# A decoder step on one core: cache pages loaded as rows of two tokens, two pages over the two halves of the partitions

## The reference, cut to what matters

```python
k_past = cache_k[l, page_table].reshape(db, past, N_HEADS, HEAD_DIM)
v_past = cache_v[l, page_table].reshape(db, past, N_HEADS, HEAD_DIM)
f_past = cache_logf[l, page_table].reshape(db, past, N_HEADS)
...
s = jnp.einsum('bqhd,bkhd->bhqk', q, k) * (HEAD_DIM ** -0.5)
s = s + c_q[...] - c_k[...]          # c = cumsum(logf) over the tokens
p = jax.nn.softmax(s, axis=-1)
o = jnp.einsum('bhqk,bkhd->bqhd', p, v)
```

## Time and profile before

| | |
|---|---|
| median of 3 runs | 2878.92 us (2878.82 to 2878.99) |
| the profiled execution | 2883.59 us, its span 2881.9 us |
| PE busy | 2639.3 us, 92% of the span |
| VectorE, ScalarE, GpSimd busy | 1429.0, 731.3 and 141.6 us |
| moved by DMA | 532.93 MB, mean 185 GB/s |
| granted TensorE clock, mean | 0.941 |

### The profile page before, as it was taken

How to read it: one execution, slowest core, us unless ns; L and a number is a source line. 1 busy time by engine, 2 the same in 40 slices (tenths; PEclk the granted TensorE clock), 3 DMA queues, 4 the chain that set the end, 5 groups by cost and what they waited for, 6 DMA issues and landing times.

```text
span 2881.9 us, 50518 instructions
## 1 busy us (share of the span) xinstructions
PE 2639.3 (92%) x19656; PEld 2326.1 (81%) x19656; DVE 1429.0 (50%) x5629; ACT 731.3 (25%) x979; POOL 141.6 (5%) x289
## 2 busy tenths in 40 slices
PE   5899899964767879998999999999999999999998
PEld 3799889851323336676999999999999999999998
DVE  4786777769777142225343434434343434343433
ACT  4332122212223341123222222222222222222221
POOL 0100000001111112200000000000000000000000
PEclk8999999985676899997999999999999999999999
DMA  6789899987999977735222222232222222322221
GB/s 238 243 290 333 315 337 343 328 302 277 359 371 359 338 263 262 250 121 174 90 89 88 88 88 89 102 103 90 88 88 89 89 89 101 104 89 88 89 88 63
DMA packets 274530, 532.93 MB, mean 185 GB/s; under 512 B 16410, under 2 KB 177787, under 8 KB 272980
## 3 DMA queue, kind: packets, MB, share of 16 engines
q1 hardware_dynamic: 218605, 376.20, 37.8%
q0 software_dynamic: 35440, 127.78, 12.1%
q10 hardware_dynamic: 20247, 25.73, 2.6%
HBM read 503.94 MB, written 24.05 MB: 183 GB/s over the span
## 4 chain that ended last, share of the span: by engine, by line
PE 77%; DMA 9%; DVE 9%; issue 2%; ACT 1%; SPq 1%; POOL 0%; POOLq 0%; ACTq 0%; DVEq 0%
PE ps L707 76%; DMA t_r<-in_cache_k 6%; DVE t_work L1777 6%; DMA t_r<-in_cache_v 1%; DMA t_wraw<-in_w_in 1%; PE ps L710 1%; DVE t_wl L1614 0%; ACT t_wh L1227 0%; DVE t_work L1614 0%; DMA t_auxW<-in_pool_w 0%; DMA t_wraw<-in_w_o 0%; DVE t_xl L1614 0%; DVE t_auxW L1614 0%; SPq L577 0%; DVE t_nmax L1915 0%
## 5 line engine op out<-in xcount | busy, mean ns | idle before, releaser
L707 PE MATMUL ps<-t_xh,t_wh 128*128 128x260 f32 (+1 forms) x4352 | 949.8, 293 | 15.4 <-DVE t_xl L1614 15.3
L707 PE MATMUL ps<-t_xh,t_wl 128*128 128x260 f32 (+1 forms) x4352 | 936.5, 291 | 0.0
L707 PE MATMUL ps<-t_xl,t_wh 128*128 128x260 f32 (+1 forms) x4352 | 935.2, 291 | 0.0
L1614 DVE TENSOR_TENSOR t_wl<-t_wraw,t_wh 128x1024 fp32r<-128x1024 f32 x376 | 460.4, 1225 | 890.9 <-ACT t_wh L1227 890.9
L1227 ACT ACTIVATE t_wh<-t_wraw 128x1024 fp32r<-128x1024 f32 x376 | 398.0, 1060 | 1654.0 <-PE ps L707 1653.8
L707 PEld LDWEIGHTS ps<-t_xh,t_wh 128*128 128x128 f32 x4352 | 685.8, 190 | 96.1 <-issue 66.2
L707 PEld LDWEIGHTS ps<-t_xh,t_wl 128*128 128x128 f32 x4352 | 686.1, 190 | 11.8
L707 PEld LDWEIGHTS ps<-t_xl,t_wh 128*128 128x128 f32 x4352 | 685.5, 190 | 8.9
L1777 DVE CUSTOM_DVE_ANT_0 t_work<-t_r,t_work 128x128 f32<-128x128 f32 x2048 | 455.2, 287 | 134.3 <-DMA t_r<-in_cache_k 121.9
L707 PE MATMUL ps<-t_hh,t_wh 128*128 128x260 f32 x1408 | 285.6, 284 | 3.4 <-issue 3.4
L707 PE MATMUL ps<-t_hh,t_wl 128*128 128x260 f32 x1408 | 284.5, 284 | 0.0
(11 more groups left out here) (256 smaller groups left out, 1205.8 us busy)
## 6 DMA issues: line engine op xcount, KB each, us to landing
t_r<-in_cache_k SPq DMA_DIRECT2D x256, 512.0 KB, 6.9
t_r<-in_cache_v POOLq DMA_DIRECT2D x228, 512.0 KB, 6.7
t_wraw<-in_w_up SPq DMA_DIRECT2D x44, 2048.0 KB, 8.0
t_wraw<-in_w_in SPq DMA_DIRECT2D x22, 2048.0 KB, 9.6
t_wraw<-in_w_down SPq DMA_DIRECT2D x22, 2048.0 KB, 7.8
t_wraw<-in_w_o SPq DMA_DIRECT2D x11, 2048.0 KB, 10.6
t_r<-in_cache_v SPq DMA_DIRECT2D x28, 512.0 KB, 6.8
scr_proj<-t_stg ACTq DMA_DIRECT2D x40, 256.0 KB, 4.6
```

The costliest lines, as they stand in the source:

```text
L707: return pe.matmul(out, lhsT, rhs, start=start, stop=stop)
L1614: return dve.tensor_tensor(out, in0, in1, op)
```

## The change

A page's 128 tokens are now seen as 64 rows of 8 KB, tokens 2q and 2q + 1 in row q (`rows_of_page`). Page n goes to 64 partitions: the lower half when its buffer's number is even, the upper half when it is odd; its 8 KB fill two neighbouring ring buffers on those partitions (`half_page`). So an even and an odd page together fill the two buffers that held them before, and a partition's first buffer holds even tokens, its second odd ones, of one page in the lower half, of the other in the upper half. Both consumers still take 128 partitions of one buffer at a time; for that both pages must have landed, and a pair's buffers are free only when both have been used. The waits follow: the consumer of an even page waits for both loads (`key_page`, `value_page`), and both loads of a pair wait for the two uses of the pair before (`key_load`, `value_places`). `biases_full` writes the biases in the same order, by four matmuls of 64 x 64 in place of a transpose. POOL waits for `x_spilled` before its first value page. Numbers, sizes and order of the loads are as before.

```diff
-    for n in range(DEC * PAGES):
+    for n in range(0, DEC * PAGES, 2):
         b = n % (2 * RING if K_END[-1] < slot_of[n] < TAIL else RING)
-        loads[b] += 1
-        places.append((b, loads[b], held.get(b, -1)))
-        held[b] = n
+        for i in range(2):
+            loads[b + i] += 1
+            places.append((b + i, loads[b + i], held.get(b, -1)))
+        held[b] = n + 1
...
+        def rows_of_page(pages, g):
+            return pages[bass.ds(g, 1), :, :].rearrange("a (q j) n -> (a q) j n", j=2)
+
+        def half_page(ring, b):
+            return ring[64 * (b % 2):64 * (b % 2) + 64, b - b % 2:b - b % 2 + 2, :]
...
                     pool.wait_ge(v_used, held + 1 + PRIME)
-                    pool.dma_start(vring[:, b, :],
-                                   v_pages[bass.ds(g, 1), :, :].rearrange("a p n -> (a p) n")).then_inc(v_loaded[b], 16)
+                    pool.dma_start(half_page(vring, b), rows_of_page(v_pages, g)).then_inc(v_loaded[b], 16)
+
+            pool.wait_ge(x_spilled, 16)
...
-            def page(ring, pages, loads, used, g, r, p):
-                sp.wait_ge(used, r * PAGES + (p + 1))
-                sp.dma_start(ring[:, p % RING, :],
-                             pages[bass.ds(g, 1), :, :].rearrange("a p n -> (a p) n")).then_inc(loads[p % RING], 16)
+            def key_load(g, n):
+                sp.wait_ge(k_used, n + 2 - n % 2)
+                sp.dma_start(half_page(kring, n % RING), rows_of_page(k_pages, g)).then_inc(k_loaded[n % RING], 16)
...
-                        last = tr(ps[:, 4 + i % 2, n * P:(n + 1) * P], lfE[:, c, h, :], P)
+                        for j in range(2):
+                            for b in range(2):
+                                last = mm(ps[64 * b:64 * b + 64, 4 + i % 2, n * P + j:(n + 1) * P:2],
+                                          lfE[:, c, h, j::2], ident[:, b::2])
...
             def value_page(r, p):
                 b, load, _ = V_PLACES[r * PAGES + p]
-                pe.wait_ge((v_loaded + k_loaded)[b], 16 * load)
+                if p % 2 == 0:
+                    for i in range(2):
+                        pe.wait_ge((v_loaded + k_loaded)[b + i], 16 * load)
...
             def key_page(r, p):
-                dve.wait_ge(k_loaded[p % RING], r * (16 * PAGES // RING) + 16 * (p // RING + 1))
+                if p % 2 == 0:
+                    for i in range(2):
+                        dve.wait_ge(k_loaded[p % RING + i], r * (16 * PAGES // RING) + 16 * (p // RING + 1))
```

More of the change, by code:

```diff
@@ L93, in value_places @@
     places, held, loads = [], {}, [0] * RING + [DEC * PAGES // RING] * RING
-    for n in range(DEC * PAGES):
+    for n in range(0, DEC * PAGES, 2):
         b = n % (2 * RING if K_END[-1] < slot_of[n] < TAIL else RING)
-        loads[b] += 1
-        places.append((b, loads[b], held.get(b, -1)))
-        held[b] = n
-    return places, max(held.get(b, -1) for b in range(RING, 2 * RING)), loads
+        for i in range(2):
+            loads[b + i] += 1
+            places.append((b + i, loads[b + i], held.get(b, -1)))
+        held[b] = n + 1
+    return places, max(held.get(b, -1) for b in range(RING, 2 * RING, 2)), loads
 V_PLACES, V_WIDE, V_LOADS = value_places()
@@ L632, in _ @@
                 for n, g in zip(kp, kg):
-                    page(kring, k_pages, k_loaded, k_used, g, *divmod(n, PAGES))
+                    key_load(g, n)
                 vp = [n for n in VALUES.get(s, []) if V_PLACES[n][0] >= RING]
@@ L641, in _ @@
                         sp.wait_ge(v_used, held + 1 + PRIME)
-                    sp.dma_start(kring[:, b - RING, :],
-                                 v_pages[bass.ds(g, 1), :, :].rearrange("a p n -> (a p) n")).then_inc(k_loaded[b - RING], 16)
+                    sp.dma_start(half_page(kring, b - RING), rows_of_page(v_pages, g)).then_inc(k_loaded[b - RING], 16)
                 n, late = divmod(s - OUT0 + 6, 4)
```

## The result

The changed kernel takes 3304.5 us (median of 6 runs, 3298.8 to 3311.2), the one before 2881.8 us (6 runs, 2878.8 to 2887.7): a ratio of 1.147, with an interval of 1.146 to 1.149. It is 15% slower. The forecast was 3147 us, 9% slower, in a range of 2930 to 3430 us.

A forecast was written before the change was run, and what follows sets the result against it. The prediction took DMA supply of key and value pages as the bound: 0.57 us more a page, divided by a 0.92 share, gives 265 us, plus 3 us for biases, 268 us; forecast 3147 us, range 2930 to 3430 us.

The forecast's parts named there:

- the forecast's own case: Page loads on half of the partitions: DMA engines partly in each other's way, 3030 to 3300 us, chance 0.48.
- full pairing: Rival for the page loads: every pair of engines meets all the time, 2.48 us a page, 3400 us, chance 0.22.
- The sign named for it: In the page loads, 8 KB packets would take about 0.5 us and not 0.31.
- With it a page costs 1.24 x 1.63 = 2.02 us, 0.57 us more than now: Page loads on half of the partitions: 8 KB rows' 1.24 us times a 1.63 slowdown, against 1.45 us now.
- The 1.63 of a load on 44 partitions: Slowdown per 512 B packet, 43 ns against 26.4, from the FFN's states' load on 44 partitions against rows leaving 128.
- 1.03 more: Upper end of the page cost: all engines work in pairs on one path at half speed, 2.48 us a page.
- No stage of the table has a share over 0.92, so I divide by that: Five page-loading stages: DMA work divided by a 0.92 share gives their new times, 265 us growth in all.
- The paired waits: Key and value page waits: put at nothing in the sum; as a rival alone, 63 us, 2942 us, chance 0.11.
- Rival "faster": Page loads: the halves don't collide, each page costs 0.21 us less, 28 us saved, 2851 us, chance 0.14.
- Keys and values come on two queues, and they will often be on different halves: Argument against full pairing, for the page loads from 229 to 1056 us; no size of its own.
- the count of 101 + 67: Third stage, 600 to 923 us: key and value pages counted there, 168 in all.
- The biases: In biases_full, 64 matmuls of 64 x 64 replace 16 transposes: 3 us more than now.

The follow-up runs named there:

- 1 MB loads: Against the changed kernel, one 1 MB load brings two neighbouring pages at fixed places onto all 128 partitions in 8 KB rows, without the page table; 2937.1 us, ratio 1.019.

## Why the prediction was right or wrong

**Right: what bounds the kernel, and where.** The prediction costed the change in time of the DMA engines by stage. The growth lies in those five stages, in the order of size that was forecast, and each has its DMA share at 0.89 to 0.97. The sign and the main cause, half of the partitions, are shown by the kernel with every second partition, which differs in nothing else that takes time and is 349 us faster. The size is less good: 15% and not 9%, and 3304 us lies 4 us above the 3030 to 3300 that the forecast's own case was given, under full pairing's 3400. The sign named for it says the same: packets of 0.56 us, between the 0.5 of the forecast and the 0.6 of full pairing.

**The mis-sized term: "With it a page costs 1.24 x 1.63 = 2.02 us, 0.57 us more than now".** A page costs 2.24 us in the changed kernel, 0.79 more; 2.28 with rows of 4 KB. The factor was not what failed. In the same stage, beside the same transfers, a page in rows of 8 KB costs 1.42 us on every second partition and 2.24 on a half: 1.58 times as much (with the engines at 0.80 there and at 0.97 here). With rows of 4 KB it is 2.28 against 1.49, 1.53 times. The 1.63 of a load on 44 partitions was near, and luckily so, since it compares a load with a store. Too low was the 1.24: it is the price of packets of 8 KB that arrive alone, 0.31 us each, and beside the other queues spread packets of 8 KB take 0.35 us. The end "1.03 more" was too far in turn. The Trainium skill ("SBUF — State Buffer", section "Door 1: The DMA port swizzle") was weighed beside this term and gave a factor of 1.58, 2.29 us a page and 3295 us as an estimate; the runs show 1.58, 2.24 to 2.34 us and 3304 us. That the time came so near is luck in part, for that sum too leaves out the next term and divides by 0.92, two errors of opposite sign. By its rule, that what counts is how many ports a load's partitions reach, every second partition reaches them all; the trace agrees, with 1.42 us a page.

**Missing from the sum: what the neighbours pay.** I counted only the pages' own packets. Put 0.79 us for each page into the stages' work and it is 145, 474, 430, 169 and 173 us; the shares measured times the windows are 147, 505, 457, 178 and 177 us. Between them lie 73 us, and at least 34 of these are other transfers' packets that take longer beside the pages'. ScalarE's queue in the third stage shows it, before, with the waits alone and in the changed kernel:

```profile
q10 hardware_dynamic: 11735, 13.67, 12.5%
```

```profile
q10 hardware_dynamic: 11591, 13.40, 10.8%
```

```profile
q10 hardware_dynamic: 11447, 13.14, 11.4%
```

40.4 us for 13.67 MB, 38.3 us for 13.40 MB, then 55.4 us for 13.14 MB: 43% more for a byte than before, in loads and stores that the change didn't touch, and the waits are not the reason. In the fifth stage SP's queue brings the same weights, before and after, and POOL's the pages:

```profile
q1 hardware_dynamic: 10592, 11.01, 19.7%
```

```profile
q0 software_dynamic: 4624, 30.40, 73.7%
q1 hardware_dynamic: 10592, 11.01, 22.0%
```

The weights take 33.5 us of 170 before and 40.5 us of 184 now, 21% more. ScalarE's queue has 27 of the 73 us over the first four stages, these weights have 7; the rest can't be split from the pages on the same queues. The pages themselves take 135.6 us for 30.40 MB, 58 pages, here: 2.34 us each, the dearest of the stages.

**"No stage of the table has a share over 0.92, so I divide by that": too low a ceiling.** The full stages run at 0.94 to 0.97 now. This error went the other way. By the prediction's own sum, 265 us for the five stages become 386 with 0.79 us a page, 465 with the 73 us of work beside it, and 419, as measured, with the measured shares in place of 0.92.

**The paired waits.** The prediction put them at nothing in the ordinary slot and priced them as a rival, alone, at 63 us and 2942 us; alone they took 74 us and 2954.8 us. The size was nearly right, the way there only in part: the slots behind a weight load were to carry it, but the time is in the first stage, 8 us, and in the second and third, 31 and 32 us, and the third has but two weight loads; the last two stages together give next to nothing. How much of the 74 us is in the 423 of the changed kernel can't be read off by adding: there the DMA engines are at 0.96, so I would expect a page asked for earlier to have stood in the queue longer. A kernel on halves without the paired waits can't be made while the consumers take 128 partitions at a time, since each buffer then holds parts of both pages; this stays open.

**Rival "faster": wrong for two reasons.** The packets didn't stay near 0.31 us, they took 0.56. And where the loads were spread (every second partition, or 1 MB loads), the row of 8 KB saved 0.07 to 0.09 us of 1.49 us a page, not 0.21: most of that difference is not the row's. Every second partition was no faster than the waits alone.

**"Keys and values come on two queues, and they will often be on different halves"**, the argument against full pairing, is worth 0.1 us a page at most: 2.24 us where POOL and SP both bring values on halves, 2.29 with spread keys beside them, 2.34 in the fifth stage, where POOL alone brings pages. Why full pairing's 2.48 us was not reached, though it builds on the low 1.24, no run here shows.

**A miscount** of 1 us: in the third stage SP also issued two value pages, which the count of 101 + 67 leaves out.

**The biases**, 3 us with ends at 0 and 6, cost 2 us of PE's work and nothing in the time that a spread of some 4 us would show.

## What to carry to other kernels

A load's place in the partitions counts for more than its width and its row size: moving the same 512 KB to one half of the partitions cost 1.5 to 1.6 times the DMA engines' time, and moving it to every second partition cost nothing. Take a packet's price from a stretch with the same traffic beside it: alone a packet of 8 KB took 0.31 us, in traffic 0.35. When the DMA engines are near full, count what a slow load does to its neighbours, not only its own packets. And a ring whose buffers are filled and freed in pairs gives its loads less lead, even where each wait looks hidden: here it cost 2.7%, most of it (58 of 80 us) by the consumer that waits for a page which it needs only later.

## What the runs showed that I had not expected

- Spread loads pay for those that are not: 1.82 us a page against 1.45, from another queue, and 43% more for a byte on ScalarE's queue.
- 64 partitions with a step of two are as fast as 128 (1.42 us against 1.49 a page).
- Rows of 8 KB against 4 KB made no difference that the runs tell, on halves (3304.5 and 3312.0 us) or spread (2955.1 and 2954.8 us).
- Moving one VectorE instruction of each slot halved the idle time for key pages (121.9 to 66.0 us) without moving the time of the kernel.
